# Changing the share of GLA work laid beside the first and the last decode sequence in one step of a hybrid decoder

## The chip, the cores and the metric

One core of a Trainium2 chip runs the whole program. The metric is the device time of one execution in microseconds (us). The median of three runs stands for a kernel.

## The reference, cut to what matters

One layer is applied to a prompt of 1024 tokens and to 8 decode sequences with 8 new tokens each. Two branches work on the same normed input: softmax attention with forgetting (FoX; for the decode sequences over 4096 cached positions read through a page table) and gated linear attention (GLA, a scan in chunks of 64). Sigmoid gates merge them.

```python
def _fox_sample(q, k_new, v_new, logf_new, cache_k, cache_v, cache_logf, page_table):
    k_past = cache_k[page_table].reshape(Bd, P, H, hd)      # P = 4096, H = 8, hd = 64
    v_past = cache_v[page_table].reshape(Bd, P, H, hd)
    ...
    p = softmax(concatenate([s_past, s_new]))               # scores plus forget sums
    o = einsum(p[..., :P], v_past) + einsum(p[..., P:], v_new)

def _gla(q, k, v, log_a, s0):                               # per chunk of 64 tokens
    q_in = qc * exp(b); k_in = kc * exp(-b)
    o = tril(q_in @ k_in.T) @ vc + q_in @ S
    S = exp(b_last) * S + (kc * exp(b_last - b)).T @ vc

y = x + (sigmoid(ma) * a + sigmoid(mb) * b) @ w_out         # ma, mb: projections too
```

## The kernel before

The program has four stages, one after the other: the inputs (`build_inputs`), the prompt's FoX attention (`build_fox`), the GLA stage (`build_gla`), and the merge (`build_merge`). The change lies in the GLA stage, which lays two independent streams of work beside each other.

The first stream is the **decode attention** of the 8 sequences (`decode_steps`, L906). A sequence has 32 key pages and 32 value pages of 256 KB, which are loaded by SP's queue into rings of 5 key buffers (`NK`) and 4 value buffers (`NV`). The steps on PE are `kt` (four transposes of a key page into a bank, L1687; ACT and DVE copy the bank out in turn, L1306 and L1180), `sc` (scores of four pages, L1702), `pt` (transposes of the weights, L1718) and `pv` (four value pages times the weights, L1735). Sequence s's keys are worked beside the values of sequence s-1: stage 0 has keys alone, stages 1 to 7 have both, and what comes after the last key page (the last scores and the last two value groups of sequence 6, and all eight value groups of sequence 7) has values alone. A value group's four loads are issued by `vstep` on SP's queue (L1190 to L1198) only when the group before it is finished on PE, since its buffers come free then. The exponentials of a sequence are one step on ACT (`exp`, L1329).

The second stream is the **GLA work** (`gla_steps`, L954): 36 projections of 1088 tokens (24 for GLA's four heads and 12 gates of the merge). Each projection has three chunks (384, 384 and 320 tokens), and each chunk is cut into four parts, called quarters here (`z` steps, L280, six matmuls each), 432 in all. Between them stand, per head, the decays (L1768), the transposes of values and keys (L1778), the chain of eight token tiles (`att` L1801, `u` L1808, `o` L1815 and L1818, `og` L1826), the samples' own steps (`satt`, `so`, `sog`) and the new sample states (`sstate`, L1858). ACT and DVE make the gates' sigmoids (L110 to L127) and split each weight tile into two parts (L255, L260). POOL's queue carries the bias rows (`prep`, L1251), the states (L1262, L1275), the gates (L1282) and the heads' outputs (L1287).

The order of both streams is written by a small planner, `schedule` (L1017). Every step has a cost in planner units (a quarter 1.0, `kt` 0.45, `sc` 1.0, `pt` 0.25, `pv` 1.1, `att` 0.3, `u` 0.55, `o` 1.0, `og` 0.25). The GLA steps before the first key page are 12 units (`LEAD`). Then the decode steps are taken in order, and after each as many GLA steps are placed as its share of the decode cost allows. The decode steps cost 270.4 units in all and the GLA steps 539.64, so each decode unit brings 527.64 / 270.4 = 1.951 GLA units. All engines and queues follow this one list, each taking the steps that concern it. The GLA steps keep their own order, and so do the decode steps; the planner only decides how they interleave. The stage ends with a clean-up of semaphores, after which the merge starts.

Of the kernel before, what the change touches and what calls it, by code (L numbers as in the profile page):

```python
# [905 lines left out]
def decode_steps():  # L906

    out = []
    for s in range(STAGES):
        a, b = s - 1, s - 2  # L910
        has_k, has_a, has_b = s < NB, 0 <= a < NB, 0 <= b < NB
        for m in range(NPG // 4):
            if has_k:
                out += [(("kt", s, 4 * m + j), 0.45) for j in range(4)]
            if m == 0:
                if has_b:
                    out.append((("pt", b, NPG // 4 - 1), 0.25))
                if has_a:
                    out += [(("sc", a, NPG // 4 - 1), 1.0), (("new", a), 0.2), (("soft", a), 0), (("exp", a), 0), (("vn_load", a), 0)]
                if has_k and s >= 1:  # L920
                    out.append((("qbd", s), 0))
            else:
                if has_k:
                    out.append((("sc", s, m - 1), 1.0))
                if has_a:
                    out.append((("pt", a, m - 1), 0.25))
            if m % 2 == 0 and s:
                out.append((("prep", s * SP + m // 2), 0))
            if m <= 1 and has_b:
                out.append((("pv", b, NPG // 4 - 2 + m), 1.1))  # L930
            if m >= 2 and has_a:
                out.append((("pv", a, m - 2), 1.1))
            if has_b:
                out += [((name, b), cost) for at, name, cost in ((1, "out", 0), (2, "od", 0.1)) if at == m]
            if has_a:
                out += [((name, a), cost) for at, name, cost in ((3, "sum", 0), (4, "pn", 0.1), (5, "pnv", 0.2)) if at == m]
    return out
# [5 lines left out]
def tile_order():  # L943

    out, m = [], 2 * KT_ - GATES_AT_END
    gates = [("m", x) for x in range(m)]
    for i in range(GH):
        mine = gates[m * i // GH:m * (i + 1) // GH]
        out += [(n, i) for n in (V0, V1, GQ, GK, G0)] + mine[:1]
        out += mine[1:] + [(G1, i)] if i < GH - 1 else [(G1, i)] + mine[1:]  # L950
    return out
# [65 lines left out]
def schedule():  # L1017


    decode, gla = decode_steps(), gla_steps()  # L1020
    total, work = sum(c for _, c in decode), sum(c for _, c in gla)
    steps, done, placed = [("prep", j) for j in range(SP)] + [("qbd", 0)], LEAD, 0.0
    while placed + gla[0][1] <= done:
        placed += gla[0][1]
        steps.append(gla.pop(0)[0])
    for step, cost in decode:
        steps.append(step)
        done += cost * (work - LEAD) / total
        while gla and placed + gla[0][1] <= done + 0.3:
            placed += gla[0][1]  # L1030
            steps.append(gla.pop(0)[0])
    steps += [step for step, _ in gla]
    order = tile_order()
    for i in range(GH):
        last = max(k for k, step in enumerate(steps) if step == ("sog", i) or step[0] == "ev_z" and order[step[1]] in ((G0, i), (G1, i)))
        steps.insert(last + 1, ("end", i))
    return steps


def build_gla(nc, ins, outs, scratch, gates, sem, sb, psum, bank, cc, vv, epsb, stream, os_fm, q_s, k_s, newb, glr):  # L1040
# [7 lines left out]
    with ExitStack() as ctx:  # L1048
# [61 lines left out]
        m_out = [sem(f"m_out{s}") for s in range(2)]  # L1110
        stream.phase(TT * 2, 0, (0, 1))
        steps = schedule()
        tiles = tile_order()
        at = {tile: n for n, tile in enumerate(tiles)}
# [1114 lines left out]
```

## Time and profile before

| | us |
|---|---|
| median of three runs | 1804.73 (1794.17 to 1809.91) |
| the profiled execution's own time | 1803.01 |
| its span | 1801.3 |
| GLA stage on PE, first projection to the last step | 520.4 to 1449.4 |
| key pages of sequence 0 | 534.3 to 598.7 |
| key pages of sequences 1 to 7 | 598.7 to 1345.5 |
| values alone | 1345.5 to 1442.9 |
| merge, first projection | 1463.5 |

How to read it: the trace is one execution. PE is TensorE's matmuls, PEld its weight loads, DVE VectorE, ACT ScalarE, POOL GpSimd, and SPq the queue of SyncE that issues the loads. Matmuls are pipelined, so their durations overlap; what a step costs is the distance from its start to the start of the next one. The granted clock 1.00 is 2.4 GHz and 0.50 is 1.2 GHz.

### The profile page before, as it was taken

How to read it: one execution, taken by the hardware profiler on the slowest of the kernel's cores; microseconds unless marked ns; L12 is line 12 of the kernel's file. 1: busy time of each engine (PE TensorE's matmuls, PEld its weight loads, DVE VectorE, ACT ScalarE, POOL GpSimd, SP SyncE). 2: the span in 40 equal slices, each digit the busy share in tenths (PEclk: the TensorE clock that was granted, in tenths of full speed). 3: DMA queues.
4: the chain of work that ended last, by engine and by line, in shares of the span. 5: the costliest groups of instructions: out<-in, count | busy, mean ns of one | idle time of the engine just before them, and what ended most of it. 6: DMA issues, size and time to landing. Idle time of an engine off the chain costs nothing. (4 is left out here: it accounts for less than half of the span.)

```text
span 1801.3 us, 35642 instructions
## 1 busy us (share of the span) xinstructions
PE 1567.7 (87%) x11525; PEld 1306.7 (73%) x11525; DVE 688.0 (38%) x1513; ACT 619.8 (34%) x1319; POOL 493.4 (27%) x935
## 2 busy tenths in 40 slices
PE   3597979889749899899989999999987658999998
PEld 2495868768448777688767887678765448888887
DVE  5326153442553344534436344453443112332211
ACT  5135242433423345324443244433333125111111
POOL 0042332423244045233243334343240012111000
PEclk9899999999879999999999999999998769999999
DMA  4111211212045467766766667766655543322143
GB/s 131 47 45 27 76 37 61 52 49 63 2 126 174 127 210 217 226 201 199 222 209 213 208 194 222 227 218 210 200 167 169 151 170 102 132 97 85 52 118 112
DMA packets 154692, 249.72 MB, mean 139 GB/s; under 512 B 37321, under 2 KB 63434, under 8 KB 153954
## 3 DMA queue, kind: packets, MB, share of 16 engines
q1 hardware_dynamic: 122978, 215.78, 38.6%
q0 software_dynamic: 31552, 31.96, 6.7%
q8 instruction: 80, 1.31, 0.3%
q14 instruction: 82, 0.67, 0.1%
HBM read 217.40 MB, written 30.22 MB: 137 GB/s over the span
## 5 line engine op out<-in xcount | busy, mean ns | idle before, releaser
L280 PE MATMUL psum<-h_hi,w_hi 128*128 128x384 f32 (+1 forms) x1536 | 556.0, 362 | 63.2 <-issue 31.8
L280 PE MATMUL psum<-h_hi,w_lo 128*128 128x384 f32 (+1 forms) x1536 | 511.4, 333 | 0.0
L280 PE MATMUL psum<-h_lo,w_hi 128*128 128x384 f32 (+1 forms) x1536 | 510.7, 332 | 0.0
L280 PEld LDWEIGHTS psum<-h_hi,w_hi 128*128 128x128 f32 x1536 | 296.7, 193 | 129.7 <-issue 116.5
L1251 POOL DMA_DIRECT2D sc<-tmp_bias x512 | 252.6, 502 | 331.4 <-PE psum L1718 327.7
L280 PEld LDWEIGHTS psum<-h_lo,w_hi 128*128 128x128 f32 x1536 | 297.1, 193 | 3.0
L280 PEld LDWEIGHTS psum<-h_hi,w_lo 128*128 128x128 f32 x1536 | 295.1, 192 | 0.0
L579 POOL DMA_DIRECT2D lfk<-in_cache_logf x256 | 136.9, 535 | 260.1 <-issue 260.1
L1687 PE MATMUL psum<-con,k_page 128*128 128x128 f32 x1024 | 155.0, 277 | 18.2 <-DVE k_t L1180 12.2
L1687 PEld LDWEIGHTS psum<-con,k_page 128*128 128x128 f32 x1024 | 122.5, 142 | 37.9 <-issue 33.6
L1306 ACT ACTIVATE k_t<-psum 128x512 f32<-128x512 f32 x128 | 75.8, 592 | 182.9 <-PE psum L1687 182.8
L1180 DVE COPY k_t<-psum 128x512 f32<-128x512 f32 x128 | 88.2, 689 | 124.6 <-PE psum L1687 123.4
L260 DVE TENSOR_TENSOR w_lo<-w_raw,w_hi 128x1024 fp32r<-128x1024 f32 x71 | 86.9, 1224 | 87.6 <-ACT w_hi L255 87.4
L255 ACT ACTIVATE w_hi<-w_raw 128x1024 fp32r<-128x1024 f32 x71 | 74.4, 1048 | 72.4 <-PE psum L280 62.1
L1735 PE MATMUL psum<-v_page,p_t 128*32 128x128 f32 x2048 | 75.8, 283 | 23.6 <-DMA v_page<-in_cache_v 22.8
L1735 PEld LDWEIGHTS psum<-v_page,p_t 128*32 128x32 f32 x2048 | 51.9, 111 | 42.0 <-DMA v_page<-in_cache_v 26.0
L2111 PE MATMUL psum<-o_hi,w_hi 128*128 128x384 f32 (+1 forms) x192 | 69.2, 360 | 0.0
L1702 PE MATMUL psum<-k_t,q_bd 128*32 128x512 f32 x512 | 68.2, 605 | 0.0
L825 PE MATMUL psum<-con,prob 128*128 128x128 f32 x288 | 44.8, 295 | 24.0 <-DVE prob_t L690 24.0
L825 PEld LDWEIGHTS psum<-con,prob 128*128 128x128 f32 x288 | 33.2, 148 | 44.2 <-issue 43.9
L809 PE MATMUL psum<-k_fm,q_fm 64*128 64x512 f32 (+3 forms) x192 | 46.9, 597 | 20.9 <-DVE nmin L682 20.9
L121 ACT ACTIVATE sig<-sig 128x384 f32<-128x384 f32 (+1 forms) x60 | 30.3, 506 | 96.9 <-DVE sig L127 96.0
(237 smaller groups left out, 2018.7 us busy)
## 6 DMA issues: line engine op xcount, KB each, us to landing
k_page<-in_cache_k SPq DMA_DIRECT2D x256, 256.0 KB, 3.5
v_page<-in_cache_v SPq DMA_DIRECT2D x256, 256.0 KB, 3.1
w_raw<-in_w_tiles SPq DMA_DIRECT2D x64, 512.0 KB, 4.5
g_pair<-tmp_gates SPq DMA_DIRECT2D x16, 544.0 KB, 4.7
sc<-tmp_bias POOLq DMA_DIRECT2D x512, 16.0 KB, 2.9
tmp_gates<-sig POOLq DMA_DIRECT2D x24, 192.0 KB, 3.7
tmp_ogla<-gate POOLq DMA_DIRECT2D x4, 1088.0 KB, 6.4
g_pair<-tmp_ogla SPq DMA_DIRECT2D x8, 544.0 KB, 4.7
```

The lines of the kernel that those rows point to most:

```text
L255: act.activation(self.hi[:, s], self.raw[:], ACT.Copy).then_inc(self.hi_set, 1)
L260: dve.tensor_tensor(self.lo[:, s], self.raw[:], self.hi[:, s].bitcast(F32), ALU.subtract).then_inc(self.lo_set, 1)
L280: m = pe.matmul(out, wt[:, s, k, :], h[:, k, t0:t0 + w], start=(k == 0 and a == 0), stop=(k == KT_ - 1 and a == 2))
L579: pool.dma_start(lfk[:, g, b * H:(b + 1) * H], ins["cache_logf"][ds(page, 1)] .rearrange("o p h -> (o p) h")).then_inc(lf_in, 16)
L825: m = pe.transpose(bank[6 + hh][:, (k - 4 * g) * P:(k - 4 * g + 1) * P], prob[hh][:, t % 2, k * P:(k + 1) * P], cc("ident"))
L1180: copy(k_t[:, p // 4 % 2, :, p % 4 * PAGE:(p % 4 + 1) * PAGE], quarters(lift_bank("kt", s, p))).then_inc(sig, 1)
L1251: pool.dma_start(sc[r0:r0 + TS, j % SLOTS, :], src.to_broadcast([TS, 512])).then_inc(sc_in[j % SLOTS], 16)
L1306: return A(out, in_, ACT.Copy)
L1687: m = pe.transpose(lift_bank("kt", s, p)[:, hp * P:(hp + 1) * P], k_page[a % NK][:, hp * P:(hp + 1) * P], cc("ident"))
L1702: m = MM(bank[5][32 * hp:32 * hp + 32, :], q_bd[:, hp, 16 * (1 - half):16 * (1 - half) + 32], k_t[:, n % 2, hp, :], start=(half == 0), sto ...
L1735: m = MM(bank[6][32 * hp:32 * hp + 32, 0:P], p_t[:, g % 2, col + 32 * hp:col + 32 * hp + 32], v_page[a % NV][:, hp * P:(hp + 1) * P], star ...
L2111: m = pe.matmul(bank[5 + c][:, 0:w], wt[:, s, k, :], v[:, k, t0:t0 + w], start=(k == 0 and a == 0), stop=(k == NBR - 1 and a == 2))
```

## The change

`schedule` multiplies the planner's cost of the decode steps before the first key page of sequence 1 by 0.75, and of those after the last key page of sequence 7 by 1.5. Nothing else is edited: every step, buffer, semaphore and tile stays.

```diff
     decode, gla = decode_steps(), gla_steps()
+    first = next(k for k, (step, _) in enumerate(decode) if step == ("kt", 1, 0))
+    last = max(k for k, (step, _) in enumerate(decode) if step[0] == "kt")
+    decode = [(step, cost * (0.75 if k < first else 1.5 if k > last else 1.0)) for k, (step, cost) in enumerate(decode)]
     total, work = sum(c for _, c in decode), sum(c for _, c in gla)
     steps, done, placed = [("prep", j) for j in range(SP)] + [("qbd", 0)], LEAD, 0.0
```

## Rows read from the trace of the kernel before

**Rows 1.** The page: busy time of the engines, and the granted clock over its 40 slices
```profile
PE 1567.7 (87%) x11525; PEld 1306.7 (73%) x11525; DVE 688.0 (38%) x1513; ACT 619.8 (34%) x1319; POOL 493.4 (27%) x935
...
PEclk9899999999879999999999999999998769999999
```

**Rows 2.** Windows by stage: length, busy time (instructions) per engine, clock, DMA share, GB/s
```profile
534.30:598.70 64.40, 63.97 (x443) 55.73 (x442) 27.19 (x47) 19.77 (x32) 25.71 (x53) 1.00 0.59 171
598.70:701.80 103.10, 98.32 (x792) 77.02 (x790) 43.92 (x102) 44.79 (x108) 30.78 (x61) 0.97 0.60 183
701.80:813.60 111.80, 104.83 (x893) 85.39 (x892) 50.97 (x114) 41.91 (x88) 40.15 (x80) 0.98 0.67 206
813.60:917.30 103.70, 102.84 (x888) 82.17 (x887) 46.26 (x108) 44.85 (x106) 38.66 (x77) 1.00 0.74 221
...
1242.40:1345.00 102.60, 95.90 (x814) 76.15 (x812) 46.72 (x108) 38.47 (x93) 37.21 (x75) 1.00 0.64 195
1345.00:1371.00 26.00, 19.63 (x206) 12.33 (x204) 12.39 (x40) 11.63 (x33) 1.35 (x3) 0.89 0.34 104
1371.00:1443.00 72.00, 48.36 (x413) 35.93 (x414) 8.42 (x22) 12.97 (x27) 6.44 (x12) 0.80 0.55 172
```

**Rows 3.** Waits of PE from 1345 to 1446 us: total, times, longest
```profile
PE psum L1735 <- DMA v_page<-in_cache_v: 22.8, 19, 3.4
PE psum L1826 <- DVE o_n L1633: 5.9, 2, 5.1
```

**Rows 4.** Timeline of PE, value products of the last two sequences
```profile
1369.00 1.94 PE L1735 MATMUL psum<-v_page,p_t 128*32 128x128 f32 x32
...
1405.40 0.43 PE L1735 MATMUL psum<-v_page,p_t 128*32 128x128 f32 x8 [0.96 <-DMA v_page<-in_cache_v]
...
1414.55 0.66 PE L1735 MATMUL psum<-v_page,p_t 128*32 128x128 f32 x8 [3.39 <-DMA v_page<-in_cache_v]
1415.48 0.66 PE L1735 MATMUL psum<-v_page,p_t 128*32 128x128 f32 x8 [0.28 <-DMA v_page<-in_cache_v]
...
1442.44 0.43 PE L1735 MATMUL psum<-v_page,p_t 128*32 128x128 f32 x8 [0.78 <-DMA v_page<-in_cache_v]
```

**Rows 5.** Value page loads: timeline of SP's queue, and the tile's times to landing
```profile
1406.61 3.65 SPq L1198 DMA_DIRECT2D v_page<-in_cache_v  x4
...
DMA to landing us min/median/max: 2.5/3.0/5.7
```

**Rows 6.** Timeline of PE, a wide projection quarter between two key pages
```profile
598.74 0.60 PE L1687 MATMUL psum<-con,k_page 128*128 128x128 f32 x4
599.09 0.42 PE L280 MATMUL psum<-h_hi,w_hi 128*128 128x384 f32 x1
...
600.23 0.49 PE L1687 MATMUL psum<-con,k_page 128*128 128x128 f32 x3
```

**Rows 7.** Timeline of PE, last chain steps and one step of each kind
```profile
1349.54 0.41 PE L1826 MATMUL psum<-con,o_n 128*128 128x128 f32 x2 [0.73 <-DVE o_n L1633]
1349.79 0.39 PE L1801 MATMUL psum<-q_in,k_in 128*128 128x128 f32 x2
...
1350.85 0.70 PE L1808 MATMUL psum<-gv_tok,gk_tok 64*128 64x256 f32 x4 [0.46 <-DVE att L1610]
1351.48 1.08 PE L1735 MATMUL psum<-v_page,p_t 128*32 128x128 f32 x32
1352.49 0.42 PE L280 MATMUL psum<-h_hi,w_hi 128*128 128x320 f32 x1
...
1353.47 0.59 PE L1815 MATMUL psum<-gv_tok,att 128*128 128x256 f32 x2
...
1354.58 0.44 PE L1718 MATMUL psum<-con,sc 128*128 128x128 f32 x2
```

**Rows 8.** Timeline of PE, key transposes of sequence 1
```profile
615.17 1.09 PE L1687 MATMUL psum<-con,k_page 128*128 128x128 f32 x4 [4.38 <-ACT k_t L1306]
```

**Rows 9.** Timeline of PE over the end of the GLA stage
```profile
1463.50 0.66 PE L280 MATMUL psum<-h_hi,w_hi 128*128 128x384 f32 x1 [14.11 <-PEq L181]
```

## The prediction

> **What bounds the kernel now.** I began with the page. PE is busy 87% of the span, and its granted clock is at full almost everywhere, except in the slices around 500 us and around 1400 us [rows 1]. The second place is the end of the GLA stage, so I cut that stage into windows [rows 2]. Beside sequence 0's keys PE is busy 63.97 of 64.40 us, so a matmul taken out there shortens the window by its own length. Beside the keys of sequences 1 to 7 it is nearly full too, with 4.8 us idle in the first window, 7.0 in the second and 0.9 in the third. From 1371 to 1443 us only 48.36 of 72.00 us are busy, at a mean clock of 0.80. The waits name the cause: value pages that had not landed (22.8 us, 19 times), and once a norm that waited behind ACT's exponentials (5.1 us) [rows 3].
>
> The timeline of these value products shows a loop of its own. The last product of sequence 6 ends at 1369.00 + 1.94 = 1370.9, the last of sequence 7 at 1442.9 [rows 4]: eight groups in 72.0 us, 9.0 each. One of them in detail: the group before ends at 1405.8, four loads are issued from 1406.6 on, the fourth some 3.3 us later, and the last product starts at 1415.5 and ends at 1416.1 [rows 4, 5]. So 10.3 us passed, with 2 to 3 us of other PE work in it. A load lands after 3.0 us at the median and 5.7 at most [rows 5]. With the median the loop would be 0.8 + 3.3 + 3.0 + 0.4 = 7.5 us; with 5.7 it is 10.2. What PE does between two groups is free as long as it is shorter than that.
>
> **The change, part by part.** First the planner. Stage 0's 21.4 decode units become 16.05, the 17.3 units behind the last key page become 25.95, the total 273.7, and the rate 527.64 / 273.7 = 1.928. Stage 0 thus gets 30.9 GLA units and not 41.8, the end 50.0 and not 33.8, and the seven stages between 446.7 and not 452.1. Laid out step by step (a step goes whole): 11 quarters leave stage 0. GLA work in the middle runs 11 units behind at first and 17.15 at the last key page. What is passed to the end is 10 quarters (27 become 37), 4 `att`, 4 `u`, 3 `o` and 3 `og`.
>
> *What PE no longer does before the last key page.* A wide quarter takes 600.23 - 599.09 = 1.14 us at full clock [rows 6], a narrow one 1353.47 - 1352.49 = 0.98 [rows 7]; two wide and one narrow give 1.09. `u` is 0.63, `o` 1.11, `og` 0.25, and `att` about 0.3 (0.39 less its overlap) [rows 7]. The sum is 10 x 1.09 + 4 x 0.63 + 3 x 1.11 + 3 x 0.25 + 4 x 0.3 = 18.7 us earlier. Stage 0 alone gives 11 x 1.09 = 12.0 of it, if its pages keep up. Its window would be 52.4 us, and its DMA share 0.59 x 64.4 / 52.4 = 0.73 (an upper value, since weight loads leave with the quarters). The window of sequence 3's keys runs at 0.74 with PE busy 99% [rows 2], so I take the full 12.0. If that cover is gone the whole of it is lost; that is the other end.
>
> *Stalls in the middle.* In stage 1 the keys wait once 4.38 us for ACT's copy [rows 8], since the exponentials of sequence 0 and gate sigmoids stand ahead of it on ACT; the clock of that window is then 0.97, another 3 us [rows 2]. After the change the exponentials meet the key projection of the first head, which asks nothing of ACT, as they do in the window of sequence 3, which has 0.9 us idle. In the later stages the chain lies 11 to 17 units later against the exponentials, sometimes better and sometimes worse. Bounds: 8 us gained, 8 lost. I take 3 gained, near half of the one stall that I can name.
>
> *From the last key page to the end of sequence 6's values* (1345 to 1371, no page loop limits PE here) [rows 2]: 4 more quarters, 3 more `u` and 3 more `att`, less the sample's `satt` and the longer `so`: 4.4 + 1.9 + 0.9 - 1.0 = 6.2 us. Three more chain steps have no key transposes beside them to fill the wait for DVE (0.46 at `u`, 0.73 at `og` [rows 7]), 1.4 us in all. The 5.1 us stall stays: its place is taken by `o` of tile 5 behind the same exponentials. Together +7.6. Bounds 5 and 11.
>
> *The eight value groups of sequence 7.* Some 10.8 us of the passed work falls here. Work between two products, with the product itself, was 4.3 us at full clock on average and becomes 5.7; the largest group has 6.3. Both lie below 7.5, so all 10.8 us hide in the waits for pages. More weight tiles and gate stores run beside the value loads: I add 1 us. Bounds: -12 (all loops at 7.5) and +11 (all at 10.4).
>
> The Trainium skill, "DMA: Bandwidth & Descriptors", section "Latency and other measured facts", speaks against the change here: memory latency grows from 0.2 us to 2 us under high load. The landings of 2.5 to 5.7 us [rows 5] agree with a spread of that kind. By that rule the loops would lie nearer to the long end. The rival on late landings is this rule.
>
> *Behind the last value group.* One more narrow quarter, 0.98 us at full and 1.96 at half clock; I take 1.5. The clean-up of 14.1 us before the merge [rows 9] is as it was, and the merge's order isn't touched.
>
> Sum: -18.7 - 3 + 7.6 + 1 + 1.5 = -11.6 us. On the profiled execution's own 1803.0 us that is 1791.4; its span ends 1.7 us below that time, and it lies 1.7 us under the median of the runs. On the median the sum gives 1793.1. I say 1792, 0.7% faster. A measurement of this kernel can tell about 1% from no change, which is 18 us.
>
> **The rivals.** *The loop gets shorter too.* Fuller groups keep PE at 2.4 GHz, which now falls after the long waits (mean 0.80 [rows 2]), and the groups start their loads sooner. If the loops go to 7.5 us, another 8 x 1.5 = 12 us go: 1780. For it: most landings are near 3.0. Against it: in all eight groups PE waited for pages, so a faster clock starts no load earlier. The Trainium skill, "TensorE: Matmul & The Clock Gate", section "HAM oscillation — how this bites in real kernels", says that waits for DMA between short bursts bring the half clock and longer bursts avoid it. The clock of 0.80 beside page waits agrees. It would remove the slow quarters, but not the page waits, so by it alone the sum stays.
>
> *The stalls return elsewhere, or the first stage doesn't shrink.* If sequence 0's page loads set its pace, 12 us are lost; if the new alignment costs 8 us and not -3, 11 are. Either gives 1802 to 1804, no change. For it: idle time in the middle differs from 0.9 to 7.0 us by alignment alone [rows 2]. Against it: rings of five pages, and the share of 0.74 seen at full pace.
>
> *Slower: value pages land late.* The place is the eight loops. If the added transfers bring every loop to the 10.3 us seen once, 11 us go, and if in every second group two pages are late and not one, 4 x 3.4 us more [rows 4]: 1792 + 11 + 14 = 1817. It decides once the loop grows by more than 1.5 us on average. Against it: the DMA share there is 0.55 [rows 2].
>
> **How the numbers follow.** Forecast (1792) 0.52; shorter loops (1780) 0.20; no change 0.20; slower (1817) 0.08. Faster by over 1% means below about 1785: the second case and a little of the first, 0.26. Slower by over 1% takes the larger part of the last case and its tail, 0.07; within 1%, 0.67. The range runs from 1775 (the short loops, with all of stage 1's stall gone) to 1809 (no change with one more stall, and half the way to late pages).
>
> **What would show it.** In the changed profile sequence 0's keys should take 52 to 53 us with PE busy over 97%; the last key page should come near 1324; the stretch from it to the end of sequence 6's values should be about 33 us and no longer 25.5; the eight groups should still take 70 to 76 us, but with PE busy some 58 of them and a clock above 0.80; page waits should fall from 22.8 to about 12 us. I am wrong if stage 0 stays above 57 us with key pages awaited, if the middle has over 10 us more idle time, or if the eight groups take under 66 or over 80 us.

## The result, and the profile after

The changed kernel takes 1771.2 us (median of 6 runs, 1762.3 to 1774.0) against 1797.7 us for the kernel before beside it. The ratio is 0.984, with a 95% interval from 0.981 to 0.987: 29 us faster by the ratio (the two medians lie 26.5 us apart), where 11.6 us were forecast and 1775 us was the low end of the range. The direction was right; the size was too small by more than half. The range was laid on the 1804.7 us that the kernel before had taken, and beside the changed kernel it took 7 us less. As a ratio the low end is 1775 / 1804.7 = 0.9835, so the measured ratio lies at that end and not far below it.

From the page of the profiled execution (1765.9 us), the engines' busy time and the granted clock, against [rows 1]:

```profile
PE 1551.2 (88%) x11525; PEld 1295.7 (73%) x11525; DVE 686.9 (39%) x1513; ACT 621.0 (35%) x1319; POOL 495.1 (28%) x935
...
PEclk7699999999979999999999999999999879999999
```

The instructions are the same 11525. The windows by stage, cut at the same steps as [rows 2], are eight windows for the keys of sequences 0 to 7, then the stretch from the last key page to the end of sequence 6's values, then the eight value groups of sequence 7:

```profile
528.90:582.80 53.90, 53.36 (x378) 44.97 (x377) 24.03 (x41) 19.62 (x32) 26.25 (x54) 1.00 0.67 192
582.80:680.20 97.40, 95.25 (x789) 76.19 (x788) 42.20 (x98) 40.79 (x95) 28.66 (x57) 1.00 0.64 191
680.20:784.90 104.70, 102.25 (x881) 80.60 (x880) 50.15 (x117) 43.03 (x96) 42.62 (x84) 1.00 0.72 224
784.90:887.10 102.20, 102.20 (x886) 83.48 (x885) 43.60 (x97) 40.81 (x93) 34.96 (x70) 1.00 0.70 212
887.10:995.40 108.30, 102.42 (x887) 81.53 (x886) 51.95 (x123) 44.80 (x102) 44.11 (x87) 1.00 0.73 223
995.40:1097.20 101.80, 101.39 (x883) 83.69 (x882) 43.16 (x96) 41.32 (x91) 34.42 (x69) 1.00 0.68 206
1097.20:1209.00 111.80, 105.29 (x891) 81.60 (x890) 53.02 (x125) 46.45 (x106) 44.65 (x88) 0.98 0.69 222
1209.00:1301.10 92.10, 91.31 (x799) 76.13 (x797) 37.98 (x83) 35.68 (x78) 30.61 (x62) 1.00 0.67 202
1301.10:1334.50 33.40, 26.81 (x233) 17.96 (x233) 15.01 (x40) 11.53 (x33) 7.47 (x15) 0.95 0.44 134
1334.50:1404.70 70.20, 53.05 (x491) 40.29 (x487) 18.69 (x53) 20.23 (x48) 6.99 (x13) 0.92 0.57 178
```

These windows say two things. At both ends the change did what was expected of it: 64.4 became 53.9 us beside sequence 0's keys; the stretch to the end of sequence 6's values went from 26.0 to 33.4 us; the eight groups stayed (72.0 and 70.2) with more PE work in them. In the middle more happened than PE's work explains. The seven windows of sequences 1 to 7 were 746 us together and are 718. By the step costs only 6.7 us of that is PE work that left (18.7 in all, 12.0 of it in stage 0).

| part of the GLA stage | forecast, us | the two traces, us |
|---|---|---|
| keys of sequence 0 | -12.0 | 64.4 to 53.9: -10.5 |
| keys of sequences 1 to 7 | -6.7 work, -3 stalls | 746.3 to 718.3: -28.0 |
| last key page to end of sequence 6's values | +7.6 | 26.0 to 33.4: +7.4 |
| the eight value groups | +1 | 72.0 to 70.2: -1.8 |
| behind them | +1.5 | 6.5 to 7.3: +0.8 |
| sum | -11.6 | -32.1 |

The profiled executions differ by 37.1 us. The other 5.0 us is in front of the GLA stage, which the change doesn't touch: PE began it at 520.4 us before and at 515.3 after.

PE's waits from the last key page to the end of the value groups, against [rows 3]:

```profile
PE psum L1738 <- DMA v_page<-in_cache_v: 9.3, 11, 3.2
PE psum L1829 <- DVE o_n L1636: 6.9, 5, 2.7
PE psum L1738 <- issue: 3.1, 2, 2.2
PE psum L1811 <- DVE att L1613: 3.0, 4, 1.4
PE psum L1818 <- DVE state L1630: 1.2, 1, 1.2
```

The page waits fell from 22.8 to 9.3 us in 11 waits (about 12 were forecast; 3.1 us more stand under issue). The waits for DVE at the chain's steps went from 6.4 to 11.1 us; more of these steps lie here now, with no key transposes beside them.

In the middle, from the first key page to the last, these are PE's largest waits for other engines, first before (of 33 us idle), then after (of 18 us):

```profile
PE psum L1687 <- DVE k_t L1180: 12.2, 9, 2.6
PE psum L1815 <- DVE state L1627: 5.4, 3, 3.7
PE psum L1687 <- ACT k_t L1306: 5.3, 2, 4.4
```

```profile
PE psum L1690 <- ACT k_t L1309: 7.5, 8, 2.5
PE psum L1829 <- DVE o_n L1636: 4.5, 3, 1.7
PE psum L1690 <- DVE k_t L1183: 3.0, 5, 1.6
```

The waits for key copies (`k_t`) fell from 17.5 to 10.5 us. Those for DVE's `state`, 5.4 us before, don't appear after.

### The profile page after: what moved, and what is told of

It is laid out like the page before. It is cut to its first block and busy times, and to the rows that moved or that the text cites. A ratio compares the mean times of both kernels' runs of the same rounds, so it can differ in the third digit from the quotient of the medians.

```text
span 1764.2 us, 35641 instructions
## 1 busy us (share of the span) xinstructions
PE 1551.2 (88%) x11525; PEld 1295.7 (73%) x11525; DVE 686.9 (39%) x1513; ACT 621.0 (35%) x1319; POOL 495.1 (28%) x935
## 5 line engine op out<-in xcount | busy, mean ns | idle before, releaser
L1738 PE MATMUL psum<-v_page,p_t 128*32 128x128 f32 x2048 | 72.2, 278 | 12.5 <-DMA v_page<-in_cache_v 9.3
L1738 PEld LDWEIGHTS psum<-v_page,p_t 128*32 128x32 f32 x2048 | 52.0, 110 | 28.5 <-issue 15.7
L825 PEld LDWEIGHTS psum<-con,prob 128*128 128x128 f32 x288 | 33.1, 148 | 43.4 <-issue 43.1
L2114 PE MATMUL psum<-o_hi,w_lo 128*128 128x384 f32 (+1 forms) x192 | 62.6, 326 | 0.0
```

Of the source, the lines that this page charges most:

```text
L825: m = pe.transpose(bank[6 + hh][:, (k - 4 * g) * P:(k - 4 * g + 1) * P], prob[hh][:, t % 2, k * P:(k + 1) * P], cc("ident"))
L1738: m = MM(bank[6][32 * hp:32 * hp + 32, 0:P], p_t[:, g % 2, col + 32 * hp:col + 32 * hp + 32], v_page[a % NV][:, hp * P:(hp + 1) * P], star ...
L2114: m = pe.matmul(bank[5 + c][:, 0:w], wt[:, s, k, :], v[:, k, t0:t0 + w], start=(k == 0 and a == 0), stop=(k == NBR - 1 and a == 2))
```

## The experiments

Each kernel was compared with the kernel before on the same chip, where that one took 1798 to 1801 us.

### One half of the change at a time

The change was cut in two. In the first kernel the order is the changed one up to the keys of sequence 7, and the 16 units meant for the end are worked beside those keys. In the second the order is that of before up to the keys of sequence 7; from there on, 16 units leave sequence 7's keys and the end gets as much work as in the changed kernel. The factors are rounded here, and the line that finds `seven` stands in both kernels.

```diff
 # middle_lag_only
-    decode = [(step, cost * (0.75 if k < first else 1.5 if k > last else 1.0)) for k, (step, cost) in enumerate(decode)]
+    seven = next(k for k, (step, _) in enumerate(decode) if step == ("kt", 7, 0))
+    decode = [(step, cost * (0.75 if k < first else 1.0122 if k > last else 1.2683 if k >= seven else 1.0)) for k, (step, cost) in enumerate(decode)]
 # end_share_only
+    decode = [(step, cost * (1.0 if k < first else 1.4819 if k > last else 0.7349 if k >= seven else 1.0)) for k, (step, cost) in enumerate(decode)]
```

> Order of all steps up to the first key page of sequence 7 as in the changed kernel; the 16 planner units that the change passes to the end are worked beside the keys of sequence 7 instead, so the stretch of values alone gets its old share (28 quarters). Theory A (the work hidden under the value loop gives about half of the gain, the other half is stalls beside the keys of sequences 1 to 6 that the new alignment avoids): the stages 1 to 6 keep their 13 us of fewer stalls, the hidden work is lost: ratio to before about 0.992 (13 to 15 us faster). Rival B (all the gain is hidden work, the stalls differ between two executions by chance): ratio 1.00, and the windows of sequences 1 to 6 as in the trace of before.

Measured: ratio 0.992 (0.9894 to 0.9946), 15 us faster. Its windows of the keys of sequences 1, 2 and 7:

```profile
582.60:680.00 97.40, 95.26 (x789) 76.22 (x788) 42.17 (x98) 40.77 (x95) 28.58 (x57) 1.00 0.62 190
680.00:784.70 104.70, 102.27 (x882) 80.59 (x880) 50.14 (x117) 43.02 (x96) 42.50 (x84) 1.00 0.70 224
...
1208.90:1322.90 114.00, 109.87 (x900) 89.29 (x898) 49.42 (x112) 43.51 (x99) 36.16 (x73) 1.00 0.58 177
```

> Order up to the first key page of sequence 7 as before; beside the keys of sequence 7 16 planner units fewer, and the end's share as in the changed kernel (36 quarters). Theory A: the work hidden at the end is 18.7 us less 8 to 10 given back: ratio about 0.994, or 0.990 if the stalls beside sequence 7's keys go as well (7 us in the traces). Rival B: the whole gain, ratio 0.984.

Measured: ratio 0.9918 (0.9886 to 0.995), 15 us faster. Its windows of the keys of sequences 1, 2 and 7, and the eight value groups:

```profile
598.60:701.60 103.00, 98.22 (x792) 77.01 (x791) 43.89 (x102) 44.83 (x108) 30.78 (x61) 0.97 0.58 183
701.60:813.20 111.60, 104.61 (x892) 85.20 (x891) 50.87 (x114) 41.91 (x88) 40.16 (x80) 0.98 0.66 206
...
1242.00:1320.40 78.40, 78.05 (x712) 63.02 (x711) 34.82 (x78) 31.39 (x72) 30.00 (x61) 1.00 0.74 229
...
1352.90:1420.80 67.90, 53.79 (x487) 39.90 (x487) 18.64 (x53) 20.22 (x48) 6.97 (x13) 0.89 0.60 184
```

The two halves give 15 us each (each to within 5 or 6 us), and 15 + 15 is near the 29 us of the change. Rival B falls on both: 1.00 and 0.984 lie outside the intervals. The windows show why: where the list is the same, a window has the same length in two executions to 0.1 or 0.2 us (97.4, 104.7 as after; 103.0, 111.6 as before). So the shorter windows in the middle belong to the order of the steps, not to the execution. In the second kernel the keys of sequence 7 run with 0.35 us idle where [rows 2] had 6.7: with less work in the list there, its stalls went too.

### One factor at a time

```diff
 # first_factor_only: 0.75 if k < first else 1.0
 # last_factor_only:  1.0 if k < first else 1.5 if k > last else 1.0
```

> Only the 0.75 ahead of sequence 1's keys; the end's share is 34.5 units (33.8 before). Theory A: no hidden work, but the lag of some 10 units in sequences 1 and 2, which shrinks to nothing by sequence 7: about half of the stalls avoided, ratio 0.994. Rival B: 1.00.

> Only the 1.5 behind the last key page; stage 0 has 40.5 units and not 41.8. Theory A: hidden work with most of its give-back, and a lag that grows from 1 to 15 units over the sequences: ratio between 0.988 and 0.994. Rival B: nearly the whole gain, 0.985.

Measured: the first factor alone 0.9975 (0.995 to 1.0001), which can hardly be told from nothing; the last alone 0.9901 (0.9867 to 0.9934), as Theory A had it. The first missed Theory A's 0.994: the lag of 10 units in sequence 1, which melts away, avoided next to no stalls in sum. (The lag is how many planner units of GLA work lie later against the keys than in the kernel before.)

The next table has, for the keys of each sequence, the window's length less PE's work by step costs like those of the prediction. This rest holds idle time and the loss at half clock, and it is an estimate, good to about 1 us a window. The two columns at the right are read from the traces without any step cost, for the seven windows together: PE's idle time, and the time at half clock, of which about half is lost.

| kernel | lag, units | 1 | 2 | 3 | 4 | 5 | 6 | 7 | sum, us | idle, us | at half clock, us |
|---|---|---|---|---|---|---|---|---|---|---|---|
| before | 0 | 7.6 | 9.4 | 0.5 | 10.3 | 0.0 | 7.2 | 7.4 | 42 | 33 | 14 |
| first factor only | 10 falling to 1 | 6.2 | 8.6 | 2.6 | 8.0 | 5.1 | 6.1 | 5.0 | 42 | 29 | 20 |
| last factor only | 1 rising to 15 | 8.3 | 11.0 | 2.1 | 5.6 | 1.2 | 6.9 | 0.7 | 36 | 25 | 14 |
| after | 11 rising to 17 | 2.3 | 4.3 | -0.8 | 7.0 | -0.6 | 9.6 | -0.3 | 22 | 18 | 3 |
| 0.70 and 1.5 | 13 rising to 17 | 2.8 | 4.8 | 1.0 | 5.0 | -0.9 | 6.6 | 0.1 | 19 | 17 | 0 |
| 0.75 and 1.6 | 11 rising to 19 | 4.5 | 8.4 | 1.5 | 6.7 | -0.5 | 4.5 | 1.2 | 26 | 19 | 7 |

The last two rows are runs of their own, neighbours of the change, made to see whether its lag or one lucky order avoids the stalls:

> 0.70 and 1.5: 2.3 us more of PE work leaves stage 0, everything beside sequences 1 to 3 lies 2 units later than in the changed kernel. If a lag of 11 to 17 units is what avoids the stalls, their sum beside sequences 1 to 7 stays near 21 us and the time near the changed kernel's; if it is the fine interleaving, step by step, the sum is anything between 20 and 42 us.

> 0.75 and 1.6: 2 us more of PE work goes to the end, where it is hidden, and the rate in the middle is 0.6% lower, so that the steps shift little by little. As for the run before: stall sum near 21 us by the lag, anything from 20 to 42 us by the fine interleaving.

Measured in one execution each: 1769.3 and 1763.5 us. The sums stay low at 19 and 26 us, while single windows move by up to 5 us (sequence 2 has 4.3 and 8.4, sequence 6 has 9.6 and 4.5). So the gain is not one lucky order: the three lists that lag by 11 units or more from sequence 1 on have 40 to 55% less of this rest than before. That the lag itself is the cause isn't shown. The 26 us lie inside what the fine order was expected to give (20 to 42), sequence 6 has more rest after than before (9.6 against 7.2) at a lag of 15, and in the list with the last factor alone it has 6.9 at a lag of 12 to 13. How a single window fares is a matter of the fine order. The window of sequence 6 in the kernel with 0.70, against the 111.8 us of the changed kernel:

```profile
1102.80:1211.70 108.90, 103.90 (x892) 81.45 (x891) 53.38 (x126) 46.45 (x106) 44.71 (x88) 1.00 0.73 229
```

### What the stalls are

Two waits of the kernel before were taken up one by one, without moving any other step: the 4.38 us wait in sequence 1 [rows 8], and one of 2.63 us in sequence 2. In sequence 1 ACT reaches the key copy only behind the exponentials:

```profile
610.71 0.72 ACT L1329 ACTIVATE sc<-sc,smst 128x512 f32<-128x512 f32 x1 [2.94 <-DVE smst L1490]
...
614.45 0.58 ACT L1306 ACTIVATE k_t<-psum 128x512 f32<-128x512 f32 x1
```

The edit gives the copies of the key pages that come then to DVE.

```diff
 # before_key_copies_dve, and the same on the changed kernel
                 by = {"pn": "act", "od": "dve"}.get(st[0], ("act", "dve")[n % 2])
+                if st[0] == "kt" and st[1] and st[2] in (4, 5, 6):
+                    by = "dve"
```

> The kernel before, with the key copies of pages 4, 5 and 6 of sequences 1 to 7 all on DVE and none on ACT, since ACT works on the exponentials then. Theory C (the stalls by alignment are mostly key banks that wait behind the exponentials): the 4.4 us wait in stage 1 and its half clock go, that window falls from 103.1 to 96 or 98 us, and the middle gets 7 to 12 us shorter. Rival D (they come from many small collisions on ACT and DVE with the chain and the gates): stage 1 falls by 3 to 7 us and the other windows move by less than 2 us, either way.

> The same on the changed kernel. Theory C: 1.7 us in stage 1 and 3 us in stage 6 go (111.8 to about 107). Rival D: under 2 us in every window.

The window of sequence 1's keys in the kernel before with this edit:

```profile
595.70:692.60 96.90, 95.64 (x791) 75.22 (x790) 45.18 (x103) 43.62 (x105) 30.91 (x61) 1.00 0.65 194
```

It falls from 103.1 to 96.9 us at full clock, and of the 4.4 us wait 0.6 is left. The change made much the same of this window (97.4), so here the cause is shown: key copies on ACT behind the exponentials. Everywhere else in the kernel before the edit did nothing or harm: sequences 2, 3, 4, 6 and 7 became 0.6 to 1.6 us longer (the window of sequence 7's keys: 104.2 us). All seven windows together became 1.5 us shorter, where Theory C had 7 to 12, and the one execution took 1799.0 us. On the changed kernel (1769.8 us, one execution) it took 1.8 us from sequence 1 (95.6) and 1.5 from sequence 6 (110.3), where Theory C had about 5. In sequence 6 the idle time stayed at about 6.5 us and the 3.4 us at half clock went. Theory C is right for sequence 1 and for little else; Theory D, with its 3 to 7 us in stage 1 and under 2 us elsewhere, fits both kernels.

The stall in sequence 2, in the trace of before: DVE around it, and the key transposes on PE that waited.

```profile
747.35 0.62 DVE L1528 TENSOR_SCALAR kdec<-psum,ba 128x384 f32<-128x384 f32 x1 [1.84 <-ACT sig L1350]
748.53 0.56 DVE L1531 TENSOR_TENSOR kdec<-kdec,sig 128x384 f32<-128x384 f32 x1 [0.56 <-ACT sig L1354]
749.13 0.96 DVE L1533 TENSOR_TENSOR_SCAN kdec<-con,kdec 128x384 f32<-128x384 f32 x1
750.00 0.53 DVE L1565 COPY k_in<-psum 128x384 f32<-128x384 f32 x1
750.45 0.68 DVE L1180 COPY k_t<-psum 128x512 f32<-128x512 f32 x1
```

```profile
751.28 1.09 PE L1687 MATMUL psum<-con,k_page 128*128 128x128 f32 x4 [2.63 <-DVE k_t L1180]
```

DVE takes its steps in the order of the list. In this decay it waits for ACT twice, scans for 0.96 us, then empties a projection bank, and only then comes the key copy that PE waits for. The edit takes the second half of the decay later:

```diff
 # before_decay_split
+        extra |= {(V0, 1, 1): [(("decay_y", i, 0), 0)], (V0, 1, 3): [(("decay_y", i, 1), 0)], (V0, 2, 1): [(("decay_y", i, 2), 0)]}
...
                     W(dve, "dc_abs", i, c + 1)
                     W(dve, "kd_turned", i, 0)
                     inc(dve.tensor_scalar(y, bank[2][:, 0:w], ba[:], 0.0, ALU.add, ALU.min), "dc_min")
+                def decay_y(i, c):
+                    t0, w = CHUNKS[c]
+                    y = kdec[:, t0:t0 + w]
                     W(dve, "dc_min", i, c + 1)
                     W(dve, "dc_ln", i, c + 1)
                     inc(T(y, y, t1[:, 0:w], ALU.subtract), "dc_y")
...
```

> The kernel before; only DVE's part of a decay is cut in two: the second half (which waits for ACT's logarithm) is taken one projection quarter later in the list, so that key copies of that quarter are no longer queued behind it. All other steps keep their order. Theory D (the middle's stalls are small head-of-line waits on DVE and ACT): the waits of 2.6 and 1.7 us in the window of sequence 2's keys go with the half clock behind the first, and it falls from 111.7 to 105 or 107 us; sequence 4 and 6 lose 1 to 2 us each. Rival C (the exponentials are what matters): below 1 us in each window.

Its windows of the keys of sequences 2, 3 and 4:

```profile
695.30:803.20 107.90, 103.30 (x892) 83.89 (x890) 50.81 (x114) 42.00 (x88) 40.32 (x80) 1.00 0.69 214
803.20:907.00 103.80, 102.93 (x889) 82.19 (x888) 46.35 (x108) 44.97 (x106) 38.83 (x77) 1.00 0.72 221
907.00:1020.10 113.10, 105.83 (x891) 84.98 (x890) 49.56 (x112) 42.60 (x91) 40.30 (x80) 0.97 0.64 202
```

Sequence 2 loses 3.9 us of its 111.8 and its half clock (the forecast was 5 to 7); 4.6 us idle stay in it. Sequence 6 loses 0.4, and sequence 4's window becomes 0.7 us longer, where 1 to 2 us less were expected of both: that part missed. The one execution took 1789.9 us, but it also began the GLA stage 5.4 us earlier. So this stall in sequence 2 is what the trace says it is, and the other windows have other collisions.

For sequences 4, 6 and 7 no run names the cause. In sequence 4 the trace of before names a path. PE waits there once for 3.68 us, for DVE's update of `state`. DVE stands in front of it at a weight tile's second part, which needs the first part from ACT, and ACT makes that only after the exponentials:

```profile
930.02 0.72 ACT L1329 ACTIVATE sc<-sc,smst 128x512 f32<-128x512 f32 x1 [1.71 <-DVE smst L1490]
...
933.77 1.04 ACT L255 ACTIVATE w_hi<-w_raw 128x1024 fp32r<-128x1024 f32 x1
```

```profile
934.84 1.23 DVE L260 TENSOR_TENSOR w_lo<-w_raw,w_hi 128x1024 fp32r<-128x1024 f32 x1 [4.85 <-ACT w_hi L255]
935.98 0.99 DVE L1627 SCALAR_TENSOR_TENSOR state<-state,e_last,psum 128x256 f32<-128x256 f32 x2
```

So the exponentials can hold PE up by another path than the key copies, which the edit of the key copies couldn't touch (its run has the same 3.7 us wait). No run tests this path.

### The loop of value pages

The prediction rested on a loop of 9 us a group: load, landing, product, and only then the next load, as the buffers are full until then. In the next pair sequence 7's odd groups are loaded into four key buffers, which are free then, so two groups are on their way at a time (S7 is the last sequence; the second part stands in `vstep`).

```diff
+                    if a // NPG == S7 and x // 4 % 2:
+                        dst, sig = k_page[x % 4], vk_in[x % 4]
...
+                    if s == S7:
+                        for x in range(4):
+                            if 4 * (g + 2) + x < NPG:
+                                load_v(s * NPG + 4 * (g + 2) + x)
+                        return
...
+                    if s == S7 - 1 and g == NPG // 4 - 1:
+                        wait_lifted(sp, "kt", S7, NPG - 1)
+                        for x in range(4):
+                            load_v(S7 * NPG + 4 + x)
...
```

> The kernel before, with sequence 7's odd value groups loaded into four key buffers that are free by then, so that two groups of values are on their way at a time. Theory (the eight last groups are a loop of load, land and product, 9 us each, with PE's other work hidden in it): the eight groups take 38 to 45 us and not 72, near PE's 34.5 us of work or the 40 us that the DMA share of 0.55 over 72 us comes to; ratio about 0.983. Rival (the transfers themselves, not the wait for free buffers, set the pace): 65 us or more, ratio above 0.995.

> The changed kernel with the same second set of value buffers. Theory: PE's 45.6 us of work now shows, the eight groups take 48 to 55 us and not 70: ratio to before about 0.972. Against the ring version of before the change then keeps the avoided stalls and stage 7 only: 15 to 20 us better, not 27; the hidden work is no longer a gain. Rival: the eight groups stay at 65 us or more and the ratio at 0.984.

Measured: 0.9835 (0.9795 to 0.9876) and 0.9693 (0.9651 to 0.9735), that is 1772.2 and 1745.2 us. The second beats both kernels. The windows of the eight value groups, first for before with the second set of buffers, then for after with it:

```profile
1369.00:1414.40 45.40, 38.28 (x413) 29.52 (x413) 8.41 (x22) 13.00 (x27) 6.47 (x12) 0.95 0.81 272
```

```profile
1333.60:1386.50 52.90, 47.41 (x487) 37.57 (x487) 18.24 (x53) 19.69 (x47) 6.43 (x12) 0.97 0.71 228
```

And PE's waits in those two windows, in the same order:

```profile
PE psum L1753 <- DMA k_page<-in_cache_v: 4.0, 5, 2.1
PE psum L1753 <- DMA v_page<-in_cache_v: 3.1, 2, 2.8
```

```profile
PE psum L1847 <- DVE o_n L1649: 4.1, 3, 2.7
PE psum L1756 <- issue: 0.9, 1, 0.9
PE psum L1829 <- DVE att L1626: 0.5, 1, 0.5
```

The loop is shown: with buffers for two groups the same pages come in 45.4 us at 272 GB/s of traffic, where 72.0 us and 172 GB/s were seen before [rows 2], and with the change's work in it there is no page wait left. The work that was hidden now costs 7.5 us (45.4 against 52.9). Over the whole stage the change takes 32.1 us off in the traces with one set of buffers, and 24.2 us with two (888.8 to 864.6 from the first key page to the last step). So the hiding is worth some 8 us in the change. The run times, with their intervals of 5 us and more, can't show so little. One expectation missed: between these two kernels I had put 15 to 20 us, and the ratios give 0.9693 / 0.9835 = 0.986, 26 us (27 by the medians). The change has most of its worth without the hiding, as its middle is worth more than I still thought.

The last kernel joins the second set of buffers, the key copies and the split decay on the changed list:

> The changed kernel with the second set of value buffers, the key copies of pages 4 to 6 on DVE, and DVE's decay in two halves. The ring alone gave 0.969. By theory D the two small edits add 3 us (stages 1 and 6) and 0 to 5 us: ratio 0.965 to 0.968. If DVE, which gets more copies, becomes the one that is late, 0.970 or more.

Measured: 0.9695 (0.9656 to 0.9734), 1742.6 us. By the run times the two small edits can't be told from nothing on top of the ring. In the traces the seven windows are 3.6 us shorter together (sequence 1 by 1.8, sequence 6 by 1.4, sequence 2 by 0.7), about the 3 us that Theory D gave to the key copies alone.

## Why the prediction was right in direction and too small

*Stage 0.* "I take the full 12.0": right to 1.5 us, 53.9 for the 52.4 us given. Its DMA share is 0.67 with PE busy 99%, so the pages kept up.

*From the last key page to the end of sequence 6's values.* +7.6 forecast, +7.4 measured, in part by luck. PE's busy time grew by 7.2 us for the 6.2 given. The idle time grew by 0.2 for the 1.4 given, since the 5.1 us stall, which was to stay, shrank to 2.5, while the other waits for DVE grew from 1.3 to 4.1.

*The value groups.* 70 to 76 us were given and 70.2 came, so the hiding worked as forecast; the -1.8 for the +1 given is within what these groups vary by from one execution to another. PE was busy 53 us for the 58 given, at a clock of 0.92: its time at half clock fell from 28.5 to 11.0 us, and more of the added work than forecast was paid by that. The ring runs show that the groups were bound by their buffers. The Trainium skill says that waits for DMA between short bursts bring the half clock ("TensorE: Matmul & The Clock Gate", "HAM oscillation — how this bites in real kernels"). The traces agree: with less waiting the clock rose from 0.80 to 0.92. The groups became hardly shorter by it (72.0 and 70.2 us). The Trainium skill's rule that latency grows under high load ("DMA: Bandwidth & Descriptors", "Latency and other measured facts") had no visible effect in the changed kernel: its loads landed after a median of 3.0 us, as before [rows 5], the longest after 6.1 where it was 5.7. In its direction the ring on the kernel before agrees: at a DMA share of 0.81 the loads into the four key buffers had a median of 4.1 us.

*The step that failed: "Stalls in the middle ... Bounds: 8 us gained, 8 lost. I take 3 gained".* In the traces it was 28.0 less 6.7, so 21 us gained. The run times say nearly the same: 26.5 to 29 us measured, less the 11.6 forecast, leaves 15 to 17 us beside the 3 taken. PE's idle time in the seven windows fell from 33.1 to 18.2 us. Its time at half clock fell from 13.7 to 3.4 us, and half of such time is lost, which makes 5 us more; together 20 us.

Two things were wrong in the step. I could name one stall and took near half of its price, though the key copies show it to be worth 6 us, clock and all. And I treated the rest as noise around nothing, with a bound of 8 us, though the four windows of [rows 2] alone held 19.4 us idle (4.8, 7.0, 0.9 and 6.7). All seven held 33 us, and with the loss at half clock 40; that was the bound for the gain. That the shift would avoid half of it couldn't be read from the rows. The signs of being wrong named only more idle time in the middle, never less. What is behind the 21 us is shown in part: key copies behind the exponentials in sequence 1 (6 us), and in sequence 2 a wait behind DVE's decay, worth 3.9 us by its split, which the changed kernel doesn't have. Why the rest went stays open; the experiments show only that it comes from the order of the steps.

*Rivals.* Shorter loops (1780) would have been nearer in time but not in cause: the loops did not shorten. "The stalls return elsewhere" as a net loss and the late pages did not happen; only sequence 6's window became longer, by 2.9 us.

## What to carry to other kernels

Where a written order interleaves two streams on in-order engines, the main engine's idle time differs between windows that do the same kind of work (0.4 to 7.3 us here), and the difference is a price of how the streams lie against each other. Add it up, with the loss at half clock, before you bound a change that shifts one stream: here half of it went. A stream of loads with too few buffers leaves waits in which other work is free, but a second set of buffers, here borrowed from a stream that had ended, was worth as much as the whole change (26 to 29 us) and added to it.

## What the runs showed that was not expected

Where the list of steps was the same, windows of 54 to 112 us came out equal to 0.2 us in separate executions. Much of the kernel's spread of about 1% lies elsewhere: PE began the GLA stage between 514.6 and 524.9 us in the 14 traces, ahead of every edit, and the eight value groups took 67.5 to 72.9 us wherever they had one set of buffers. One trace therefore tells an effect of 1 us in a window whose order is fixed, where the 95% intervals of the run times here reach 5 to 7 us to either side.
